# Hybrid attention and expert-retrieval layer: head 0's query by token tile, the last four modulation pieces on TensorE

## What is computed

```python
mod = (silu(c) @ w_ada + b_ada)                  # w_ada is 2048 x 12288
sh1, sc1, g1, sh2, sc2, g2 = split(mod, 6)
h  = rmsnorm(x) * (1 + sc1) + sh1                # then projections, two kinds of attention, w_o
x  = x + g1 * mixed
h2 = rmsnorm(x) * (1 + sc2) + sh2
q  = (h2 @ w_peer_q).reshape(tokens, 8 heads, 2, 128)
s1, s2 = q[..., 0, :] @ keys1.T, q[..., 1, :] @ keys2.T    # 128 keys each
v1, i1 = top_k(s1, 16);  v2, i2 = top_k(s2, 16)
best, pos = top_k(v1[:, None] + v2[None, :], 16)           # 16 experts of 16384 per token and head
u, vv = peer_u[expert], peer_v[expert]                     # 2048 floats each
y  = sum over 8 heads x 16 experts of softmax(best) * gelu(u . h2) * vv
x  = x + g2 * y;  out = rmsnorm(x)
```

## Time and profile before

| | |
|---|---|
| median of 3 runs | 1827.88 us (1827.41 to 1830.53) |
| the profiled execution's own time | 1827.87 us |
| span in the profile | 1824.8 us |
| PE busy | 1473.6 us, 81% |
| DVE busy | 1141.1 us, 63% |
| POOL busy | 618.2 us, 34% |
| DMA | 716.43 MB, mean 393 GB/s |

### The profile page before, as it was taken

How to read it: one execution, slowest core, us unless ns; L and a number is a source line. 1 busy time by engine, 2 the same in 40 slices (tenths; PEclk the granted TensorE clock), 3 DMA queues, 4 the chain that set the end, 5 groups by cost and what they waited for, 6 DMA issues and landing times.

```text
span 1824.8 us, 13714 instructions
## 1 busy us (share of the span) xinstructions
PE 1473.6 (81%) x4834; PEld 829.2 (45%) x4834; DVE 1141.1 (63%) x1562; ACT 349.2 (19%) x697; POOL 618.2 (34%) x625
## 2 busy tenths in 40 slices
PE   2979999999898987787777777768877777777776
PEld 1559987887787632232332323224332322222332
DVE  5868886789789755545555555538455555554445
ACT  3004343853201211011110111102011101010110
POOL 0001011001055863444344343428543443433341
PEclk9979999999999999999999999998999999999999
DMA  9999998569799999999999999999999999999995
GB/s 339 386 389 405 400 355 318 210 242 391 273 403 414 421 421 422 422 422 421 422 421 422 421 421 422 422 412 413 421 422 423 422 422 421 422 422 422 421 422 231
DMA packets 138241, 716.43 MB, mean 393 GB/s; under 512 B 11158, under 2 KB 15436, under 8 KB 63692
## 3 DMA queue, kind: packets, MB, share of 16 engines
q0 software_dynamic: 82976, 604.02, 80.1%
q1 hardware_dynamic: 55212, 111.77, 16.6%
HBM read 713.65 MB, written 2.10 MB: 392 GB/s over the span
## 4 chain that ended last, share of the span: by engine, by line
DMA 58%; DVE 14%; PE 14%; POOL 6%; issue 4%; ACT 2%; SPq 0%; DVEq 0%; POOLq 0%; ACTq 0%
DMA u_rows<-in_peer_u,expert 50%; DVE u_rows L1751 6%; PE ps L768 4%; DMA v_rows<-in_peer_v,expert 4%; POOL u_rows L665 3%; DVE first_acc L454 3%; POOL v_rows L665 3%; PE ps L925 3%; PE ps L762 2%; DMA ada_first<-in_w_ada 2%; PE ps L425 2%; DMA u_rows<-in_peer_v,expert 1%; DVE ada_acc L293 1%; DMA ada_late<-in_w_ada 1%; PE ps L732 1%
## 5 line engine op out<-in xcount | busy, mean ns | idle before, releaser
L1021 PE MATMUL ps<-v_rows,diag 128*128 128x512 f32 x1960 | 907.8, 610 | 266.7 <-DMA v_rows<-in_peer_v,expert 252.4
L1751 DVE SCALAR_TENSOR_TENSOR u_rows<-u_rows,h 128x2048 f32<-128x2048 f32 x256 | 587.1, 2293 | 519.6 <-DMA u_rows<-in_peer_u,expert 517.2
L1021 PEld LDWEIGHTS ps<-v_rows,diag 128*128 128x128 f32 x1960 | 359.9, 192 | 813.1 <-issue 584.8
L665 POOL DMA_INDIRECT u_rows<-in_peer_u,expert x256 | 283.8, 1109 | 622.6 <-DVE u_rows L1751 576.3
L665 POOL DMA_INDIRECT v_rows<-in_peer_v,expert x249 | 286.1, 1149 | 97.0 <-issue 78.6
L1350 ACT ACTIVATE diag<-ident,hidden 128x128 f32<-128x128 f32 x250 | 89.3, 395 | 848.7 <-PE ps L1021 534.0
L293 DVE SCALAR_TENSOR_TENSOR ada_acc<-ada_late,cact,ada_acc 128x2048 f32<-128x2048 f32 x57 | 133.8, 2348 | 19.4 <-DMA ada_late<-in_w_ada 18.3
L279 POOL DMA_DIRECT2D ada_late<-in_w_ada x61 | 32.4, 532 | 305.3 <-DVE ada_acc L293 263.7
L990 PE MATMUL ps<-h2T,ring 128*128 128x256 f32 x512 | 117.3, 389 | 6.7 <-DMA ring<-in_w_peer_q 6.7
L990 PEld LDWEIGHTS ps<-h2T,ring 128*128 128x128 f32 x512 | 99.3, 196 | 20.9 <-DMA ring<-in_w_peer_q 7.1
L454 DVE SCALAR_TENSOR_TENSOR first_acc<-ada_first,cact,first_acc 128x1024 f32<-128x1024 f32 x60 | 77.1, 1284 | 15.3 <-DMA ada_first<-in_w_ada 9.9
(11 more groups left out here) (273 smaller groups left out, 1258.0 us busy)
## 6 DMA issues: line engine op xcount, KB each, us to landing
ada_late<-in_w_ada POOLq DMA_DIRECT2D x61, 1024.0 KB, 7.7
ada_first<-in_w_ada SPq DMA_DIRECT2D x64, 512.0 KB, 11.6
ring<-in_w_in SPq DMA_DIRECT2D x10, 2048.0 KB, 23.6
ring<-in_w_o SPq DMA_DIRECT2D x8, 2048.0 KB, 19.9
ring<-in_w_peer_q SPq DMA_DIRECT2D x8, 2048.0 KB, 20.1
opened<-in_w_in SPq DMA_DIRECT2D x8, 1024.0 KB, 13.0
u_rows<-in_peer_u,expert POOLq DMA_INDIRECT x256, 32.2
v_rows<-in_peer_v,expert POOLq DMA_INDIRECT x249, 34.2
```

What stands on the lines that cost most here:

```text
L665: nc.gpsimd.indirect_dma_start(buf[:, :], None, table, bass.IndirectOffsetOnAxis(ap=expert[:, q, k:k + 1], axis=0)).then_inc(done, 16)
L1021: ins = nc.tensor.matmul(ps[:, c, :], diag[i % len(diag)][:, :], buf[:, 512 * c:512 * c + 512], start=(n % HALF_SLOTS == 0), stop=last)
L1751: nc.vector.scalar_tensor_tensor(out=buf[:, :], in0=buf[:, :], scalar=1.0, in1=h2[:, q // H, :], op0=ALU.mult, op1=ALU.mult, accum_out=hid ...
```

## The change

1. **Head 0 by token tile, operands exchanged.** `first_head(t, lo, hi)` takes the 128 tokens of tile t as the stationary block and 256 columns of `w_peer_q` as the moving one: 16 products for each tile. The result has tokens on partitions, so ACT copies it to `q0`, PE transposes it (`first_turned`), ACT copies that to `pq`, PE scores (`first_score`), ACT copies 256 scores. Job 0 needs tile 0 alone.
2. **The last four pieces, 92 to 95, on PE.** `last_products` multiplies each 128x128 block of a piece with one column of `cact`, 16 products to a piece, 64 in all, into bank 7. They stand four at a time behind each of the last ten products of tile 1, and in groups of six among the transposes that follow. `ada_cols(5)` moves behind head 1's products (from the middle of head 2) and adds `ada_acc`, now 12 pieces, to the same columns.
3. **Steps re-placed.** DVE sums pieces 86 to 88, does job 0's retrieval, waits until the first gather has been issued, then sums 89 to 91. The first three gathers wait for 16, 32 and 48 of the 64 products, the next three for the sums of 89, 90 and 91; the buffers of `u_rows` are given in another order for that. ACT's copy of tile 1's first scores waits for all 64 products.
4. **Later retrievals re-placed.** Job 1 stays in slots 0 to 7; job j of 2 or more now runs in the 16 slots from 8 + 16 (j - 2), so job 2 takes slots 8 to 23. `exponent(q)` moves by one job on ACT.

```diff
-    LAST_PIECES = 6 * KC - 3
+    LAST_PIECES = 6 * KC - 4
...
+    def last_products(lo, hi):
+        for p in range(lo, hi):
+            i, b = divmod(p, KC)
+            part, kc = divmod(LAST_PIECES + i, KC)
+            if p == 0:
+                nc.tensor.wait_ge(ada_last_loaded, 16 * len(ada_last))
+            ins = nc.tensor.matmul(ps[:, 7, KC * part + b:KC * part + b + 1], ada_last[i][:, P * b:P * b + P],
+                                   cact[:, kc:kc + 1], start=(p == 0), stop=False, skip_group_check=True)
+            if b == KC - 1:
+                ins.then_inc(ada_columns, 1)
...
                 if n < 3:
-                    pool.wait_ge(ada_steps, LAST_PIECES - EARLY)
+                    pool.wait_ge(ada_columns, 4 + n)
                 elif n < 6:
-                    pool.wait_ge(ada_steps, LAST_PIECES - EARLY + n - 2)
+                    pool.wait_ge(ada_steps, LAST_PIECES - EARLY - 5 + n)
                 if n == 6:
-                    pool.wait_ge(ada_columns, 4)
+                    pool.wait_ge(ada_columns, 8)
...
+                    ins = nc.tensor.matmul(ps[:, unit[f"fq_{t}"][0], 0:2 * P], h2T[:, ch, P * t:P * t + P], w0[:, ch, 0:2 * P],
+                                           start=(ch == 0), stop=(ch == KC - 1))
...
+            first_head(0, 0, KC)
+            first_head(1, 0, 3)
+            first_turned(0)
+            first_head(1, 3, 6)
+            first_score(0)
+            for ch in range(6, KC):
+                first_head(1, ch, ch + 1)
+                last_products(4 * ch - 24, 4 * ch - 20)
+            token_rows(0)
+            last_products(40, 46)
+            first_turned(1)
+            token_rows(1)
+            last_products(46, 52)
+            first_score(1)
+            token_rows(2)
+            last_products(52, 58)
+            token_rows(3)
+            last_products(58, 64)
+
-            for u in range(H):
+            for u in range(1, H):
...
-                    if u == 2 and m == 5:
+                    if u == 1 and m == 7:
                         ada_cols(5)
...
+            def first_scores_out(t):
+                if t == 1:
+                    act.wait_ge(ada_columns, 7)
...
-                job, slots = (1 + k // 8, 8) if q == 0 else (q + 2, TOPK)
+                job, slots, k2 = (1, 8, n) if n < 8 else (2 + (n - 8) // TOPK, TOPK, (n - 8) % TOPK)
...
-            for k in g2_steps[:-3]:
+            for k in g2_steps[:3]:
                 ada_sum(k)
             for part in range(RETRIEVAL):
                 retrieve(part, 0)
-            for k in g2_steps[-3:]:
+            dve.wait_ge(first_issued, 1)
+            for k in g2_steps[3:-4]:
                 ada_sum(k)
```

More of the change, by code:

```diff
@@ L262, in build @@
     ada_late_loaded = [nc_sem(f"ada_late{b}_loaded") for b in range(3)]
-    ada_last_loaded = [nc_sem(f"ada_last{b}_loaded") for b in range(3)]
-    LAST_PIECES = 6 * KC - 3
+    ada_last_loaded = nc_sem("ada_last_loaded")
+    LAST_PIECES = 6 * KC - 4
     def ada_place(k):
         if k >= LAST_PIECES:
-            return ada_last[k - LAST_PIECES], ada_last_loaded[k - LAST_PIECES], 0
+            return ada_last[k - LAST_PIECES], ada_last_loaded, 0
         j = k - EARLY
@@ L366, in build @@
     before_retrieval = list(used)
-    plan([f"p{u}" for u in range(8)], [0, 1, 2, 3])
-    plan([f"sc{u}" for u in range(8)], [4, 5])
+    plan(["fq_0", "fq_1", "p0_0", "p0_1"] + [f"p{u}" for u in range(1, 8)], [0, 1, 2, 3])
+    plan(["sc0_0", "sc0_1"] + [f"sc{u}" for u in range(1, 8)], [4, 5])
     plan([f"h2_{u}" for u in range(8)], [6])
@@ L679, in gather_u @@
                     pool.wait_ge(dots, n - len(u_rows) + 1)
-                gather(n, buf, landed, peer_u[0])
+                gather(n, buf, landed, peer_u[0], first_issued if n == 0 else None)
             def gather_v(n):
@@ L1309, in std, with first_query, first_query_turned @@
                 nc.scalar.activation(st[:, 2 + t:3 + t], st[:, 2 + t:3 + t], ACT.Sqrt).then_inc(y_std, 1)
-            for u in range(H):
+            def first_query(t):
+                empty(nc.scalar.copy(q0[:, t, :], full(act, f"fq_{t}")[:, 0:2 * P]), f"fq_{t}")
+            def first_query_turned(t):
+                empty(nc.scalar.copy(pq[:, 0, :, P * t:P * t + P], full(act, f"p0_{t}")[:, 0:2 * P].rearrange("p (s t) -> p s t", s=2)),
+                      f"p0_{t}")
+            def first_scores_out(t):
+                if t == 1:
+                    act.wait_ge(ada_columns, 7)
+                empty(nc.scalar.copy(s_all[:, t, 0:2, :], full(act, f"sc0_{t}")[:, 0:2 * P].rearrange("p (s n) -> p s n", s=2)),
+                      f"sc0_{t}")
+            first_query(0)
+            first_query_turned(0)
+            first_scores_out(0)
+            first_query(1)
+            token_rows_out(0)
+            first_query_turned(1)
+            for u in range(1, 4):
+                token_rows_out(u)
+            first_scores_out(1)
+            for u in range(1, H):
                 if u == 4:
@@ L1730, in retrieve @@
                 t, h = divmod(q, H)
-                if part == 0 and t == 0:
-                    copied(dve, f"sc{h}")
+                if part == 0 and (t == 0 or h == 0):
+                    copied(dve, f"sc{h}" if h else f"sc0_{t}")
                 if part < 8:
@@ L1796, in serve @@
                     ada_finish(5)
-                job, slots = (1 + k // 8, 8) if q == 0 else (q + 2, TOPK)
+                job, slots, k2 = (1, 8, n) if n < 8 else (2 + (n - 8) // TOPK, TOPK, (n - 8) % TOPK)
                 if job < QJOBS:
-                    for part in range(RETRIEVAL * (k % slots) // slots, RETRIEVAL * (k % slots + 1) // slots):
+                    for part in range(RETRIEVAL * k2 // slots, RETRIEVAL * (k2 + 1) // slots):
                         retrieve(part, job)
```

64 lines of the change are left out of this document (39 added, 25 removed).

## The result

The changed kernel takes 1847.05 us (median of 4 runs, 1845.61 to 1848.08) against 1828.88 us (4 runs, 1827.41 to 1830.53) for the kernel before: ratio 1.0103, 95% interval 1.0092 to 1.0115. It is slower by about 18 us; 1844 us was forecast. The profiled execution took 1848.08 us with a span of 1845.5 us, 20.7 us more than the span of before.

The account below looks back on a forecast made before the run. DMA's full rate from 591 us on bounds the kernel; the end moves as gather 30 does, less what DMA catches up: 26.5 - 2.0 - 5.0 - 3 = +16.5 us, 1844 us, range 1827 to 1851 us.

Parts of the forecast that it names:

- DVE sets the pace ahead of gather 30: Between dot 1 and dot 16 DVE idles only 4.1 us; the next eight slots take 2.69 us each.
- Part 1: Start of the gathers: head 0 by tile lets gather 0 start at 494.1 us, 9.0 us earlier.
- Part 2: PE ahead of head 1: 64 one-column products take 13.9 us; head 1 starts at 503.8 us at full clock, against 491.85 us.
- the faster rival: Weave on PE: woven one-column products cost nothing and the clock holds; -6 us, 1822 us, chance 0.10.
- Part 3: PE's clock halves in the weave at 491 us, bounds 487 to 495 us; head 1 starts at 516.6 us.
- From head 1 to dot 1: Head 1's start to its scores takes 24.6 us; DVE waits, and dot 1 starts at 542.3 us, 26.5 us later.
- (a): Credit on dots 2 to 16: their 2.0 us of waits for rows are gone.
- (b): Credit on slots 8 to 15: they carry half of job 2's retrieval instead of all, 5.0 us less.
- (c): Credit at gather 30: about 4 us of transfers queued on DMA instead of 7 us, so 3 us.
- The signs: Trace marks: DVE idle some 20 us behind dot 0, gather 6 near 536 us, gather 30 near 610 us, among others.
- What makes dot 1 late stays late, but for three credits: From dot 1 to the end: 26.5 us of lateness less 2.0, 5.0 and 3 us leaves +16.5 us.
- The other edits cost nothing: Rest of the change: an early `ada_last` load, jobs ending two slots ahead and a moved exponent have no cost it could price.

Follow-up runs that it names:

- experiment 6: The kernel before with only the later retrievals re-placed as in the change: 1828.62 us, ratio 1.0002.
- experiment 5: The change with the later retrievals back in their old slots, nothing else: 1850.61 us, ratio 1.0130 to the kernel before.
- experiment 2: The change with 60 of the 64 one-column products left out, every wait kept: 1823.38 us, ratio 0.9975 to the kernel before.
- experiment 4: The change with the last four pieces summed on DVE again and `ada_cols(5)` back inside head 2: 1824.08 us, ratio 0.9988 to the kernel before.
- experiment 8: The version of experiment 4 with the later retrievals back in their old slots: 1824.87 us, ratio 0.9988 to the kernel before.
- experiment 9: The change with `ada_cols(5)` right behind head 1's score instead of ahead of it: 1845.04 us, ratio 1.0082 to the kernel before.
- experiment 3: The change with job 1's retrieval in slots 4 to 7 instead of 0 to 7: 1840.25 us, ratio 1.0076 to the kernel before.
- Experiment 1: The change with 18 unused 256-column products added among the one-column ones: 1837.5 us, ratio 1.0057 to the kernel before.
- experiment 7: The version of experiment 4 with `ada_cols(5)` right behind head 1's score: 1825.31 us, ratio 0.9988 to the kernel before.

## Why the prediction was right, by its own steps

The direction, the mechanism (a lost clock, late scores, a DVE that waits for them, an idle DMA) and the time were right, 1844 us against 1847.05 us. The sum was made for the span of one profiled execution, +16.5 us, and there it was 20.7 us, 4.2 us more; the medians differ by 18.2 us. Up to dot 1 two terms were too small by 3.8 us together, and two waits were not priced.

- **The bound.** DMA at 421 GB/s to the end, and the end set by what has been moved before: right. But "DVE sets the pace ahead of gather 30" does not hold of the kernel before in the sense that counts: DVE releases gather 30 there, and with half a retrieval less on DVE gather 30 came 2.8 us earlier behind head 0's first product and the time stayed (experiment 6, +0.3 us). DVE's pace reaches the end only where the DMA has gaps, as in the change (experiment 5).
- **Part 1.** Gather 0 at 494.53 us, forecast 494.1 us. The 9 us do not come through: gather 2 waits for 48 of the 64 products, which stand under the half clock. The prediction counted what the DMA loses only from dot 1 on and did not price this wait. Without the products, what is left of the change is worth 3 to 4 us (experiments 2, 4, 8).
- **Part 2.** In the weave at full clock a group of four one-column products and its wide one recur every 1.32 us (488.00 - 486.68), where 0.217 x 4 + 0.43 = 1.30 us was taken. Right: the groups and the wide products add up, so next to nothing of one lies beside the other, and the faster rival falls.
- **Part 3.** The clock fell at 489.2 us, forecast 491 us within 487 to 495. Head 1 started at 518.42 us, forecast 516.6 us; the earlier fall is the difference, as each microsecond of full clock lost there costs one more. That 491 us was so near is partly luck: with the same stream on PE up to there the fall came 5.2 us behind the first one-column product in the change, 5.8, 5.9 and 8.8 us in experiments 9, 5 and 3. Experiment 1 shows the cause. The rule of the Trainium skill ("TensorE: Matmul & The Clock Gate", section "Why this matters for your kernels") on idle gaps does not describe it: PE was busy in every microsecond from 483.6 us on and lost its clock all the same. With 18 more wide products in the same stretch it kept it.
- **From head 1 to dot 1.** This is the other term that was mis-sized. Forecast 24.6 us to the scores, measured 545.03 - 518.42 = 26.6 us: head 1's products 16.3 us for 15.8, `ada_cols(5)` 4.6 us for 4.0, the four products of head 2 3.55 us for 2.6, score and copy 2.1 us for 2.2. The clock fell a second time inside `ada_cols(5)`, at 537.0 us (1.00 from 534.7 to 537 us, 0.50 from there to 543 us), and all four products of head 2 ran at half speed. With part 3's 1.8 us dot 1 came 30.35 us late instead of 26.5 us.
- **Dot 0.** It waited 14.11 us for ACT's copy of `h`, since the transposes behind the weave ran late too. The prediction did not name this. It cost nothing, as the next step waited 25.82 us for the scores.
- **Credits.** (a) and (b), 7.0 us in the forecast, were 6.5 us up to dot 23 (66.2 us from dot 1 instead of 72.7 us, where dot 23 started at 588.46 us); experiment 5 measures (b) by itself as 4.8 us on DVE, 5.0 forecast, of which 3.6 to 4.1 us reach the end. Gather 30 came another 0.8 us late, as POOL was still issuing the one before. (c), the backlog, is what is then left between gather 30 and the span, 24.7 - 20.7 = 4.0 us, 3 forecast; no run measures it by itself. So 30.35 - 6.5 + 0.8 - 4.0 = 20.7 us for the span, where 16.5 us were forecast; by medians it is 18.2 us. That the medians differ by less than the spans is scatter, and makes the forecast look better: the profiled execution of the change was the slowest of four, 1.0 us above their median, and that of the kernel before 1.0 us below its own.
- **The signs.** Of those that the prediction named, the gap of DVE behind dot 0 is 25.8 us (forecast some 20), gather 6 at 539.8 us (536) and gather 30 at 615.7 us (610): late by 3.8 and 5.7 us against the forecast; dot 1 is late by 3.8 us.
- **What the sum hid.** "What makes dot 1 late stays late, but for three credits" gave the right size for this kernel and is no rule. Experiment 9 took 7.4 us off dot 1 and off gather 30 and 2.0 us off the time: there credit (c) was -0.5 us (17.3 - 17.8). So gather 30 is a poor mark where the stretch ahead of it differs; the bytes up to 640 us account for both kernels.
- **"The other edits cost nothing."** Right for the re-placed retrievals in a kernel whose DMA is full (experiment 6).

Not tried: a place for the 64 products in which they delay neither the gathers nor head 1. Experiment 2 is 0.7 us faster than experiment 4, within the scatter of ten runs each, so little is to be expected of it.

## What to carry to other kernels

Where one stretch of a kernel runs at the full DMA rate to its end, measure an edit ahead of it by the bytes moved up to a fixed time, not by when one transfer starts: a step that comes earlier while the queue is full brings nothing (experiments 6 and 7), and one that lets an idle DMA start brings what the DMA then moves and no more (experiment 9: 7.4 us earlier, 1.1 MB more, 2.0 us). Where two kernels are compared by one profile each, look first at whether the clock fell at the same place in both (experiment 3). Work moved to an engine that seems to have room has to be priced by who waits behind it there. One-column products on PE cost as much again through the clock here, so keep enough wide products among them, see in the trace that the clock stays, or leave such sums where they were.

## What was new about the hardware

- PE's clock fell from 2.4 to 1.2 GHz at 489.2 us with no idle time, when one wide product of 0.43 us stood between groups of four one-column ones (1.32 us a round). With two wide products in each of the ten rounds (1.76 us), and two ahead of each six one-column products in the tail, it stayed at 2.4 GHz for the whole 28 us. Where in the weave it falls differs from one execution to the next: 5.2, 5.8, 5.9 and 8.8 us behind the first one-column product in four of them with the same stream.
- The issue of an indirect gather took 1.9 to 3.1 us when one of DVE's 128 x 2048 operations was already running as it began, and 0.94 to 1.15 us otherwise, also where such an operation began with the issue or during it. In the kernel before, from 512 to 760 us, 28 issues began inside a dot product and took 1.90 to 3.06 us; 30 began ahead of one that they met, or within 0.03 us of its start, and took 0.94 us; 52 met none and took 0.94 to 1.15 us. Gather 3 begins with dot 0 (511.15 to 513.42 us) and takes 0.94 us; gather 4 begins in the middle of it and lasts until 0.9 us behind its end:

```profile
511.17 0.94 POOL L665 DMA_INDIRECT u_rows<-in_peer_u,expert  x1 [0.30 <-issue]
512.41 1.90 POOL L665 DMA_INDIRECT u_rows<-in_peer_u,expert  x1 [0.30 <-issue]
```

In the other profiles three issues that began within 0.3 us of a dot's end were short too (1.08 us at 540.72 us in experiment 9). The longer issue looks like a bound, POOL issuing without a pause for 60 us in experiment 4, and was none (experiment 7).
